# Modulation units issued later: two per item in layer 0, four in layer 1, five per head in layer 2, four per head in layer 3

## The chip, the cores and the metric

The program runs on one core of one Trainium2 chip. The metric is the device time of one execution in microseconds (us), as the median of the runs.

## What is computed

The reference is a stack of two blocks of two layers each, over 256 image tokens and 256 context tokens of width 1024. Layers 0 and 1 belong to the first block (grouped attention, pooling and Fourier branches, SwiGLU), layers 2 and 3 to the second (differential attention over 8 heads, a depthwise convolution of 31 taps, gates, squared-ReLU MLP). Before everything a layer does, it needs its *modulation*: six vectors of 1024 numbers, computed from a conditioning vector alone.

```python
for i in range(DEPTH):
    ...
    mod_x = (sc @ w_ada[i] + b_ada[i])[:, None, :]      # w_ada[i]: 1024 x 6144
    sh1, sc1, ga1, sh2, sc2, ga2 = jnp.split(mod_x, 6, axis=-1)
    hx = rms_norm(x, g_mix[i]) * (1.0 + sc1) + sh1
    ...                                                  # attention and the other branches
    x = x + ga1 * (mx @ w_out[i])
    fx = rms_norm(x, g_ffn[i]) * (1.0 + sc2) + sh2
    x = x + ga2 * swiglu(fx, w_gate_up[i], w_down[i])
```

In the second block an attention weight is the difference of two softmax maps per head, and q and k of a head are normalised and rotated first. The last layer of each block updates the image tokens only, so that layers 1 and 3 have 256 query columns and layers 0 and 2 have 512.

## The kernel before

`plan()` writes all steps into one list; each engine then walks this list and emits its own part, so that an engine's order of work is the order of the list, and semaphores do the rest. Layers are counted from 0 here, as in the code.

**Weights.** Every weight block is 128 columns by up to 1024 rows (step `wb`). ScalarE rounds it into `w_hi` (line 1272), VectorE makes the rest `w_lo` (line 1517), and TensorE does three matmuls for each 128 rows (lines 1130 to 1132). All weights come through one ring of four buffers `raw`, in one stream of DMAs that SyncE issues in order (line 1074); an entry is fetched when the entry four places ahead of it has been consumed.

**Modulation units.** The matrix `w_ada` of a layer is read in 3 banks of 16 units; a unit is one ring entry of 512 KB and four short matmuls (line 1110), which read it as it lands. A bank sums up in a PSUM bank of its own and is then transposed and finished by VectorE (lines 1566 to 1580). The plan says where the units stand: `layer_first` takes a number of units per attention item in layers 0 and 1 (`pump`), `layer_second` takes up to 10 per head in layer 2 and distributes them over a head's groups by the table `UNITS_IN`, and the norm before the MLP (`gap`) and the MLPs of layers 0 and 1 take the remaining 8 and 8 of one bank. Before the change every unit of layer 3 was done by the end of layer 2, and layer 3 had none.

**Attention.** `attend` interleaves the items (128 queries of one head). Of one item the TensorE order is: scores `S` (line 1207, into `sc`), transposes `T` of the item before (line 1217, into `pt`), fill work, the values product `PV` of the item before (line 1231 or 1233, into `pv`), more fill work. Scores go through VectorE (maximum, line 1726), ScalarE (exponential, line 1413) and VectorE (normalising: line 1741 in the first block, 1747 in the second) before they can be transposed. ScalarE copies the transposes (line 1422). The fill work of a head in layers 2 and 3 is a table of `groups`, 8 for four items in layer 2 and 4 for two items in layer 3: the next head's q, k and v blocks, their norms, and the end of the head before.

**The norms of q and k.** `query_sum` (called through `q_norm`) is a matmul of squares into `aux` (line 1161), a rotation matmul (line 1165), two ScalarE reads of `aux` (lines 1372 and 1374; the second one says that `aux` is free), and VectorE work. `qk_norm` (called through `k_norm`) is a matmul into the same `aux` (line 1140), which must wait for that, and a rotation matmul (line 1145). Its result is spread by 16 short matmuls (line 1155), which the rope of k (line 1701) reads.

**The end of a head.** Behind the spread rows come `PV`, the transpose of v (line 1172), the transposes of the finished head (line 1239), and the first scores of the next head. VectorE does taps of the convolution in between (line 1790). In layers 1 and 3 VectorE may hold a block's `w_lo` back (`split_due`) until the next block or the next modulation unit stands in the list.

Of the kernel before, what the change touches and what calls it, by code (L numbers as in the profile page):

```python
# [29 lines left out]
NT = 512  # L30
# [12 lines left out]
UNIT = 1024  # L43
ADA_BANKS = 3
LAYERS = 4
UNITS_IN = (0, 1, 1, 1, 1, 2, 2, 2)
LAM_INIT = [0.8 - 0.6 * float(np.exp(-0.3 * i)) for i in range(2)]


# [48 lines left out]
def plan():  # L98
# [9 lines left out]
    def signal(name, n=1):  # L108
        c[name] = c.get(name, 0) + n
        return name, c[name]  # L110

    def take(resource, slots, release):
        n = used.get(resource, 0)
        used[resource] = n + 1
        slot = n % slots
        before = last.get((resource, slot))
        last[resource, slot] = release
        return slot, before
# [7 lines left out]
    def step(kind, **kw):  # L126
        s = Step(kind=kind, i=counts.get(kind, 0), **kw)
        counts[kind] = s.i + 1
        steps.append(s)
        return s  # L130

    def after(name):
        return name, c.get(name, 0)
# [28 lines left out]

    def turn_place(s, q):

        if q.layer == 2:
            s.pt, s.pt_free = "pv", last.get(("pv", 0))
            last["pv", 0] = signal("turn_read")
        else:
            s.pt, s.pt_free = take("pt", 2, signal("turn_read"))
# [79 lines left out]
    def turn_probs(item):  # L249

        s = step("T", item=item)
        s.pt = []
        for h in range(2 if item.first else 1):
            ev = signal("pt_read")
            pt, free = take("pt", 2 if item.first or item.layer == 3 else 1, ev)
            pts, pts_free = take("pts", 2, None)
            s.pt.append(Step(bank=pt, free=free, ev=ev, slot=pts, slot_free=pts_free))
        last["e", item.e] = s.pt[-1].ev
        item.pt = s.pt
# [49 lines left out]
    def transpose(src, made, v_slot, v_free):  # L309

        s = step("tt", src=src, n=made.n, ready=made.rel, slot=v_slot, slot_free=v_free)
        s.ev = signal("pt_read")
        s.pt, s.pt_free = take("pt", 1 if made.layer == 2 else 2, s.ev)
        last[src, 0] = s.ev
        return s

# [19 lines left out]
    def ada_list(layer, banks=range(ADA_BANKS)):  # L336
        return [(layer, b, h, k) for b in banks for h in range(2) for k in range(KD)]
# [252 lines left out]
    def layer_second(layer, ada_head=(), first=(), gap=()):  # L590
# [29 lines left out]
        def conv_gate(t):  # L620
            g = w("w_cg", t, n, "sg", func=ACT.Sigmoid)
            g.qg, g.qg_free = take("sgl", 2, None)
            glu.append(g)

        def conv_value(t):
            g = glu[t]
            glu[t] = w("w_ca", t, n, "glu", other=g, free=last.get(("cz", 0)))
            last["sgl", g.qg] = glu[t].rel
# [131 lines left out]
        ada_left = [lambda a=a: ada(*a, psum="pt") for a in ada_head]  # L760
        q_block, k_block, q_norm, q_done, v_block, k_norm, k_made, k_done, v_turn = head_work(0)
# [14 lines left out]
        for h in range(8):  # L776
            its = q_items(False, h % 2, h % 2, h % 2, h, both, (held["kr", h].done, held["qr", h].done, held["vt", h].ev),
                          held["qr", h].norm)
            for it in its:
                it.layer = layer  # L780
                it.oslot = h % 2


            def mark(h=h):
                held["o", h - 1] = after("o_ready")
            q_block, k_block, q_norm, q_done, v_block, k_norm, k_made, k_done, v_turn = head_work(h + 1) if h < 7 else [lambda: None] * 9
            total, scale, turn_back, low = out_norm(h - 1) if h else [lambda: None] * 4
            mark = mark if h else lambda: None
            if both:
                groups = [[q_block], [], [mark, q_norm, q_done, k_block], [total], [k_norm, k_made, v_block, k_done],  # L790
                          [scale, v_turn], [turn_back, low], []]
            else:
                groups = [[q_block], [k_block, q_norm, q_done], [mark, total, k_norm, k_made, v_block, k_done, scale],
                          [v_turn, turn_back, low]]
            if h < 2:
                if both:
                    groups[6].append(lambda h=h: conv_gate(2 + h))
                    groups[7].append(lambda h=h: conv_value(2 + h))
                else:
                    groups[3].append(lambda h=h: conv_pair(2 + h))  # L800
            if h == 6:
                groups[-1].append(conv_add)
            if h == 7:
                g, p = conv_gate_of, conv_product
                if both:
                    parts = [[g(0), conv_mean, conv_centre], [conv_squares, g(1), conv_rstd], [conv_scale, g(2)], [g(3)],
                             [p(0), g(4)], [p(1), g(5)], [p(2), g(6)], [p(3), g(7)]]
                else:
                    parts = [[g(0), conv_mean, conv_centre, conv_squares, g(1), conv_rstd], [conv_scale, g(2), g(3)],
                             [p(0), g(4), p(1), g(5)], [p(2), g(6), p(3), g(7)]]  # L810
                for a, b in zip(groups, parts):
                    a += b
            ada_now = ada_left[:10]
            ada_left = ada_left[len(ada_now):]
            for j, g in enumerate(groups):
                slots = (7 - h) * len(groups) - j - 1
                if slots > 0:
                    g.append(lambda slots=slots: conv_taps(taps_due(slots, len(groups))))
                a, b = sum(UNITS_IN[:j]), sum(UNITS_IN[:j + 1])
                g += ada_now[a:b]  # L820
            attend(its, [lambda g=g: [f() for f in g] for g in groups])
            last["kT", h % 2] = after("scores_done")

            last["v", h % 2] = ("pv_done", c.get("pv_done", 0) + 1)
        attend_last()
        held["o", 7] = after("o_ready")
        total, scale, turn_back, low = out_norm(7)
# [15 lines left out]
        s = step("merge", n=n)  # L843
# [7 lines left out]
        for m in range(KD):  # L851
            s = wb(layer, "w_out2", m, "act", 0, KD, n, "resid", gate=16)
# [8 lines left out]
    r = rstd(D, NT, after("square_added"))  # L861
# [1 line left out]
        ada(*a)  # L863
    newton(r)
    step("lam")
    layer_first(0, ada_list(0, [1, 2]) + ada_list(1, [0]), 3, ada_list(1, [1])[:8], r)
    ffn(0, NT, ada_list(1, [1])[8:], NT)
    layer_first(1, ada_list(1, [2]), 2, ada_list(2, [0])[:8])
    ffn(1, NX, ada_list(2, [0])[8:], NT)
    layer_second(2, ada_list(2, [1, 2]) + ada_list(3)[:40], gap=ada_list(3)[40:])  # L870
    ffn(2, NT, [], NT)
    layer_second(3)
    ffn(3, NX, [], 0)


# [21 lines left out]
    r = 0  # L897
# [6 lines left out]


PLAN = plan()


# [1079 lines left out]
```

How the kernel before makes its waits and increments, by code:

```python
        def wait(eng, what):  # L1033
            if what is not None and what[1] > 0:
                eng.wait_ge(S[what[0]], what[1])
# [1 line left out]
        def wait_landed(eng, r):  # L1038
            eng.wait_ge(landed[r % RAW], 16 * (r // RAW + 1))
# [7 lines left out]
        @block.sync  # L1047
# [11 lines left out]
                    continue  # L1059
                if r == RAW:
                    sp.dma_start(x[:, :, :], xin).then_inc(S["x_in"], 16)
                    sp.dma_start(consts[:, 0:5 * P], const[:, 0:5 * P]).then_inc(S["const_in"], 16)
                if r == 16:
                    sp.dma_start(consts[:, 5 * P:], const[:, 5 * P:]).then_inc(S["const_in"], 16)
                    sp.dma_start(small[:, :, :], wsmall).then_inc(S["small_in"], 16)
                if r >= RAW:
                    before = raw_entries[r - RAW]
                    if before[0] == "w":
                        sp.wait_ge(S["lo_ready"], before[1] + 1)
                    else:
                        sp.wait_ge(S["ada_used"], before[1].used[1])
                n = UNIT if kind == "ada" else blocks[what][3] * P
                src = stream[offset:offset + P * n].rearrange("(p n) -> p n", p=P)
                sp.dma_start(raw[:, r % RAW, 0:n], src).then_inc(landed[r % RAW], 16)
                offset += P * n
                r += 1
            for s in steps[-KD:]:
                wait(sp, s.rel)
                sp.dma_start(out[s.m * P:(s.m + 1) * P, :], x[:, s.m, 0:NX]).then_inc(S["stored"], 16)
            sp.wait_ge(S["stored"], 16 * KD)
```

## Time and profile before

| what | value |
|---|---|
| median of 3 runs | 2478.14 us (2475.3 to 2478.62) |
| profiled execution, its own time | 2479.97 us |
| its span | 2478.2 us |
| TensorE matmul busy | 2331.5 us, 94% |
| TensorE weight loads busy | 1897.6 us, 77% |
| VectorE busy | 1323.9 us, 53% |
| ScalarE busy | 1040.2 us, 42% |
| HBM read | 332.58 MB, 135 GB/s over the span |

PE is the matmul side of TensorE and PEld its weight loads, DVE is VectorE, ACT is ScalarE, SP is SyncE. Matmuls are pipelined: a row's duration holds the way through the array too, so what a group costs is read from its start to the start of the group behind it. Attention runs from about 90 to 208 us in layer 0, 675 to 745 in layer 1, 1047 to 1400 in layer 2 and 1975 to 2200 in layer 3. The granted clock (PEclk) is 1.00 at 2.4 GHz and 0.50 at 1.2 GHz.

### The profile page before, as it was taken

To read this page: it belongs to the slowest core of one execution; us is meant where nothing else is said; L and a number is where in the kernel's file an instruction comes from. 1 tells how busy PE (TensorE), PEld (TensorE's weight loads), DVE (VectorE), ACT (ScalarE), POOL (GpSimd) and SP (SyncE) were. 2 spreads that over 40 slices of the span, in tenths; PEclk is the share of its full clock that TensorE was granted. 3 is DMA by queue.
4 is the path that set the end of the run, shared out by engine and by line. 5 is a ranking of instruction groups with operands and counts; after the bars stand their busy time and mean duration, and the time that the engine had idled before them with its cause. 6 is when DMAs were issued, how large, how long until landed. Compare 5 with 4: busy or idle time off the path is not lost.

```text
span 2478.2 us, 35757 instructions
## 1 busy us (share of the span) xinstructions
PE 2331.5 (94%) x14174; PEld 1897.6 (77%) x14174; DVE 1323.9 (53%) x2254; ACT 1040.2 (42%) x1966; POOL 33.2 (1%) x40
## 2 busy tenths in 40 slices
PE   5999899999888998899999999899999899998999
PEld 2656688888657998767666787688888787798999
DVE  4444433333655555567776434444344578756665
ACT  3343422222544444444445523423323465664543
POOL 0300000000200000000000000000000000000000
PEclk9999999999999999899999999899999899999999
DMA  7465433323345665144554322323223221154554
GB/s 268 155 223 168 142 110 102 110 94 111 111 166 183 194 207 182 65 145 155 194 182 151 110 95 85 126 96 107 89 94 103 74 96 60 60 162 145 173 189 141
DMA packets 94885, 335.96 MB, mean 136 GB/s; under 512 B 10624, under 2 KB 12672, under 8 KB 94464
## 3 DMA queue, kind: packets, MB, share of 16 engines
q1 hardware_dynamic: 94720, 333.67, 40.9%
q8 instruction: 114, 1.87, 0.3%
q14 instruction: 51, 0.42, 0.1%
HBM read 332.58 MB, written 1.05 MB: 135 GB/s over the span
## 4 chain that ended last, share of the span: by engine, by line
PE 85%; DVE 5%; ACT 4%; DMA 4%; issue 2%; SPq 0%; ACTq 0%; DVEq 0%
PE out L1130 24%; PE out L1131 24%; PE out L1132 24%; DMA raw<-stream 4%; PE sc L1207 2%; PE pt L1217 1%; PE pt L1110 1%; PE pv L1233 1%; PE aux L1155 1%; PE out L1110 1%; ACT w_hi L1272 1%; PE pv L1231 1%; PE aux L1140 1%; PE sc L1110 1%; DVE w_lo L1517 1%
## 5 line engine op out<-in xcount | busy, mean ns | idle before, releaser
L1130 PE MATMUL out<-act_hi,w_lo 128*128 128x512 f32 (+1 forms) x2272 | 804.2, 354 | 35.0 <-DVE act_lo L1681 26.4
L1131 PE MATMUL out<-act_lo,w_hi 128*128 128x512 f32 (+1 forms) x2272 | 789.7, 348 | 0.0
L1132 PE MATMUL out<-act_hi,w_hi 128*128 128x512 f32 (+1 forms) x2272 | 788.5, 347 | 0.0
L1272 ACT CAST w_hi<-raw 128x1024 fp32r<-128x1024 f32 (+2 forms) x444 | 452.3, 1021 | 428.2 <-PE out L1132 418.6
L1517 DVE TENSOR_TENSOR w_lo<-raw,w_hi 128x1024 fp32r<-128x1024 f32 (+2 forms) x444 | 529.8, 1196 | 172.5 <-ACT w_hi L1272 171.8
L1130 PEld LDWEIGHTS out<-act_hi,w_lo 128*128 128x128 f32 x2272 | 438.8, 193 | 100.2 <-issue 42.7
L1132 PEld LDWEIGHTS out<-act_hi,w_hi 128*128 128x128 f32 x2272 | 438.1, 193 | 53.0
L1131 PEld LDWEIGHTS out<-act_lo,w_hi 128*128 128x128 f32 x2272 | 438.6, 193 | 50.3
L1130 PE MATMUL out<-mix_hi,w_lo 128*128 128x512 f32 (+1 forms) x1120 | 377.8, 337 | 4.4 <-DVE mix_lo L1754 1.7
L1131 PE MATMUL out<-mix_lo,w_hi 128*128 128x512 f32 (+1 forms) x1120 | 376.3, 336 | 0.0
L1132 PE MATMUL out<-mix_hi,w_hi 128*128 128x512 f32 (+1 forms) x1120 | 376.2, 336 | 0.0
L1130 PEld LDWEIGHTS out<-mix_hi,w_lo 128*128 128x128 f32 x1120 | 212.5, 190 | 30.5 <-issue 4.7
L1132 PEld LDWEIGHTS out<-mix_hi,w_hi 128*128 128x128 f32 x1120 | 212.5, 190 | 21.9
L1131 PEld LDWEIGHTS out<-mix_lo,w_hi 128*128 128x128 f32 x1120 | 212.6, 190 | 21.7
L1616 DVE SCALAR_TENSOR_TENSOR x<-out,mods,x 128x256 f32<-128x256 f32 x216 | 97.8, 480 | 199.0 <-PE out L1132 199.0
L1591 DVE TENSOR_TENSOR e_t<-e_t,out 128x512 f32<-128x512 f32 (+1 forms) x44 | 24.4, 554 | 230.1 <-PE out L1132 225.1
L1790 DVE SCALAR_TENSOR_TENSOR stage<-stage,vecs 128x512 f32<-128x512 f32 (+1 forms) x240 | 139.1, 613 | 1.8
L1413 ACT ACTIVATE e_t<-sc,smax,rq 128x512 f32<-128x512 f32 (+1 forms) x144 | 100.8, 706 | 55.7 <-DVE smax L1729 55.3
L1598 DVE TENSOR_TENSOR e_t<-e_t,out 128x512 f32<-128x512 f32 (+1 forms) x64 | 35.5, 555 | 138.0 <-ACT e_t L1336 137.9
L1336 ACT ACTIVATE e_t<-out 128x512 f32<-128x512 f32 (+1 forms) x64 | 31.5, 493 | 146.1 <-PE out L1132 146.1
L1726 DVE TENSOR_REDUCE smax<-sc 128x2 f32<-128x1024 f32 (+1 forms) x72 | 75.1, 1042 | 29.9 <-PE sc L1207 29.4
L1422 ACT COPY p_t<-pt 128x512 f32<-128x512 f32 (+1 forms) x96 | 47.1, 517 | 100.0 <-PE pt L1217 100.0
(193 smaller groups left out, 1886.1 us busy)
## 6 DMA issues: line engine op xcount, KB each, us to landing
raw<-stream SPq DMA_DIRECT2D x604, 512.0 KB, 3.6
raw<-stream SPq DMA_DIRECT2D x16, 384.0 KB, 3.1
raw<-stream SPq DMA_DIRECT2D x16, 256.0 KB, 2.7
x<-xin SPq DMA_DIRECT2D x1, 2048.0 KB, 11.8
consts<-const SPq DMA_DIRECT2D x1, 1344.0 KB, 8.0
x<-ctx SPq DMA_DIRECT2D x1, 1024.0 KB, 5.9
out<-x SPq DMA_DIRECT2D x8, 128.0 KB, 1.7
consts<-const SPq DMA_DIRECT2D x1, 320.0 KB, 11.6
```

The source lines that it names most:

```text
L1110: ins = nc.tensor.matmul(ada_bank[32 * q:32 * q + 2, s.half * NX:(s.half + 1) * NX], cv[:, s.layer // 2, s.k, :], u[:, q], start=(s.k == 0 ...
L1130: nc.tensor.matmul(ps, wl, xh, start=(k == 0), stop=False)
L1131: nc.tensor.matmul(ps, wh, xl, start=False, stop=False)
L1132: ins = nc.tensor.matmul(ps, wh, xh, start=False, stop=(k == s.nk - 1))
L1207: ins = nc.tensor.matmul(scb[h][:, 0:b - a], q_t[rows, it.qslot, it.c0:it.c0 + P], k_t[rows, it.kslot, a:b], start=True, stop=True)
L1272: nc.scalar.copy(w_hi[:, number % HL, 0:n], raw[:, place[number] % RAW, 0:n]).then_inc(S["hi_ready"], 1)
L1413: ins = nc.scalar.activation(e_t[:, 2 * it.e + h, 0:n], scb[h][:, 0:n], ACT.Exp, scale=rq[:, it.qslot, j:j + 1], bias=smax[:, it.e, h:h + ...
L1422: nc.scalar.copy(p_t[:, t.slot, 0:n // P, :], ptb[t.bank][:, 0:n].rearrange("p (t n) -> p t n", n=P))\
L1517: nc.vector.tensor_tensor(w_lo[:, number % HL, 0:n], raw[:, place[number] % RAW, 0:n], w_hi[:, number % HL, 0:n].bitcast(F32), ALU.subtrac ...
L1616: ins = nc.vector.scalar_tensor_tensor(out=x[:, s.m, cols], in0=ps[:, cols], scalar=mods[:, s.layer, s.gate + s.m, h:h + 1], in1=x[:, s.m, ...
L1726: link(nc.vector.reduce_max(smax[:, it.e, :], scores_of[:, :, 0:n], AX_X))
L1790: nc.vector.scalar_tensor_tensor(out=dst, in0=src, scalar=w, in1=dst, op0=ALU.mult, op1=ALU.add)\
```

## The change

Every bank after the first ones is read later: in sum 16 units (one bank of layer 1) leave the attention of layer 0 for layer 1's, and 32 units (two banks of layer 3) leave the attention of layer 2 for layer 3's. The table of layer 2 gets 5 units a head instead of 10, layer 3 gets a table of its own with one unit in each of a head's four groups, and the units of layers 2 and 3 now both take the PSUM bank `pt1`. So layer 3 has one bank left for the transposes, the rotations of q and k go to the back half of `pv`, and the norm of the next q moves one group later, behind the scores of the second item.

```diff
--- before.py
+++ after.py
@@ -43,7 +43,7 @@
 UNIT = 1024
 ADA_BANKS = 3
 LAYERS = 4
-UNITS_IN = (0, 1, 1, 1, 1, 2, 2, 2)
+UNITS_IN = {2: (0, 1, 0, 1, 0, 1, 1, 1), 3: (1, 1, 1, 1)}
 LAM_INIT = [0.8 - 0.6 * float(np.exp(-0.3 * i)) for i in range(2)]
 
 
@@ -162,7 +162,7 @@
 
     def turn_place(s, q):
 
-        if q.layer == 2:
+        if q.layer >= 2:
             s.pt, s.pt_free = "pv", last.get(("pv", 0))
             last["pv", 0] = signal("turn_read")
         else:
@@ -252,7 +252,7 @@
         s.pt = []
         for h in range(2 if item.first else 1):
             ev = signal("pt_read")
-            pt, free = take("pt", 2 if item.first or item.layer == 3 else 1, ev)
+            pt, free = take("pt", 2 if item.first else 1, ev)
             pts, pts_free = take("pts", 2, None)
             s.pt.append(Step(bank=pt, free=free, ev=ev, slot=pts, slot_free=pts_free))
         last["e", item.e] = s.pt[-1].ev
@@ -310,7 +310,7 @@
 
         s = step("tt", src=src, n=made.n, ready=made.rel, slot=v_slot, slot_free=v_free)
         s.ev = signal("pt_read")
-        s.pt, s.pt_free = take("pt", 1 if made.layer == 2 else 2, s.ev)
+        s.pt, s.pt_free = take("pt", 1 if made.layer >= 2 else 2, s.ev)
         last[src, 0] = s.ev
         return s
 
@@ -790,7 +790,7 @@
                 groups = [[q_block], [], [mark, q_norm, q_done, k_block], [total], [k_norm, k_made, v_block, k_done],
                           [scale, v_turn], [turn_back, low], []]
             else:
-                groups = [[q_block], [k_block, q_norm, q_done], [mark, total, k_norm, k_made, v_block, k_done, scale],
+                groups = [[q_block], [k_block], [mark, q_norm, total, q_done, k_norm, k_made, v_block, k_done, scale],
                           [v_turn, turn_back, low]]
             if h < 2:
                 if both:
@@ -810,13 +810,13 @@
                              [p(0), g(4), p(1), g(5)], [p(2), g(6), p(3), g(7)]]
                 for a, b in zip(groups, parts):
                     a += b
-            ada_now = ada_left[:10]
+            ada_now = ada_left[:sum(UNITS_IN[layer])]
             ada_left = ada_left[len(ada_now):]
             for j, g in enumerate(groups):
                 slots = (7 - h) * len(groups) - j - 1
                 if slots > 0:
                     g.append(lambda slots=slots: conv_taps(taps_due(slots, len(groups))))
-                a, b = sum(UNITS_IN[:j]), sum(UNITS_IN[:j + 1])
+                a, b = sum(UNITS_IN[layer][:j]), sum(UNITS_IN[layer][:j + 1])
                 g += ada_now[a:b]
             attend(its, [lambda g=g: [f() for f in g] for g in groups])
             last["kT", h % 2] = after("scores_done")
@@ -863,13 +863,13 @@
         ada(*a)
     newton(r)
     step("lam")
-    layer_first(0, ada_list(0, [1, 2]) + ada_list(1, [0]), 3, ada_list(1, [1])[:8], r)
-    ffn(0, NT, ada_list(1, [1])[8:], NT)
-    layer_first(1, ada_list(1, [2]), 2, ada_list(2, [0])[:8])
+    layer_first(0, ada_list(0, [1, 2]), 2, ada_list(1, [0])[:8], r)
+    ffn(0, NT, ada_list(1, [0])[8:], NT)
+    layer_first(1, ada_list(1, [1, 2]), 4, ada_list(2, [0])[:8])
     ffn(1, NX, ada_list(2, [0])[8:], NT)
-    layer_second(2, ada_list(2, [1, 2]) + ada_list(3)[:40], gap=ada_list(3)[40:])
+    layer_second(2, ada_list(2, [1, 2]) + ada_list(3, [0])[:8], gap=ada_list(3, [0])[8:])
     ffn(2, NT, [], NT)
-    layer_second(3)
+    layer_second(3, ada_list(3, [1, 2]))
     ffn(3, NX, [], 0)
```

The order of instructions below is that of one head in the middle of a layer. The first piece is TensorE in layer 3, around the second item of a head (line 1110 is a unit, 1161 and 1165 belong to the norm of q, 1140 and 1145 to that of k, 1207 are the scores, 1217 the transposes):

```order
 L1132 MATMUL out<-act_hi,w_hi 128x512
-L1161 MATMUL aux<-consts,sq 128x2 x2
-L1165 MATMUL pt<-qg,consts 128x256
+L1110 MATMUL pt<-raw,cv 2x256 x4
 L1207 MATMUL sc<-k_t,q_t 128x512 x2
 L1217 MATMUL pt<-consts,e_t 128x128 x4
+L1161 MATMUL aux<-consts,sq 128x2 x2
+L1165 MATMUL pv<-qg,consts 128x256
 L1140 MATMUL aux<-consts 128x2 x4
-L1145 MATMUL pt<-qg,consts 128x256
+L1145 MATMUL pv<-qg,consts 128x256
 L1130 MATMUL out<-act_hi,w_lo 128x512
```

The norm of q stood ahead of the scores and now stands directly ahead of the norm of k, with nothing of TensorE between the two. The same place on ScalarE (1413 are the exponentials of the second item, 1372 and 1374 read `aux`):

```order
+L1433 ACTIVATE o_t,o_ss<-pv 128x128
+L1434 COPY o_t<-pv 128x128
+L1422 COPY p_t<-pt 128x512
+L1413 ACTIVATE e_t,ssum<-sc,smax,rq 128x512 x2
 L1372 ACTIVATE q_y<-aux,eps 128x4
 L1374 ACTIVATE q_ms<-aux,eps 128x4
 L1375 ACTIVATE q_y<-q_y 128x4
 L1376 ACTIVATE q_sq<-q_y 128x4
-L1433 ACTIVATE o_t,o_ss<-pv 128x128
-L1434 COPY o_t<-pv 128x128
-L1422 COPY p_t<-pt 128x512
-L1413 ACTIVATE e_t,ssum<-sc,smax,rq 128x512 x2
```

The reads of `aux` moved from ahead of the exponentials to behind them. The end of a head in layer 3 on VectorE (1701 is the rope of k behind the spread rows, 1747 the normalising of the second item), before:

```order
L1669 SCALAR_TENSOR_TENSOR n_r<-n_sq,n_y 128x8
L1517 TENSOR_TENSOR w_lo<-raw,w_hi 128x1024
L1701 TENSOR_TENSOR k_t<-qg,aux 128x512
L1767 SCALAR_TENSOR_TENSOR o_sq<-o_ms,o_sq 128x2
L1768 SCALAR_TENSOR_TENSOR o_r<-o_sq,o_y 128x2
L1770 TENSOR_TENSOR consts<-consts,o_r 128x256
L1790 SCALAR_TENSOR_TENSOR stage<-stage,vecs 128x256 x3
L1744 RECIPROCAL srec<-ssum 128x1
```

and of the change:

```order
L1669 SCALAR_TENSOR_TENSOR n_r<-n_sq,n_y 128x8
L1701 TENSOR_TENSOR k_t<-qg,aux 128x512
L1767 SCALAR_TENSOR_TENSOR o_sq<-o_ms,o_sq 128x2
L1768 SCALAR_TENSOR_TENSOR o_r<-o_sq,o_y 128x2
L1770 TENSOR_TENSOR consts<-consts,o_r 128x256
L1790 SCALAR_TENSOR_TENSOR stage<-stage,vecs 128x256 x3
L1517 TENSOR_TENSOR w_lo<-raw,w_hi 128x1024
L1744 RECIPROCAL srec<-ssum 128x1
```

The `w_lo` of a block moved from ahead of the rope to between the taps and the normalising, since a unit now stands there. The end of a head in layer 2 on TensorE, before:

```order
L1155 MATMUL aux<-consts,n_r 64x128 x8
L1110 MATMUL pt<-raw,cv 2x256 x4
L1233 MATMUL pv<-v_t,p_t 128x128 x4
L1172 MATMUL pt<-consts,vf 128x128 x4
L1110 MATMUL pt<-raw,cv 2x256 x8
L1207 MATMUL sc<-k_t,q_t 128x256 x2
L1217 MATMUL pt<-consts,e_t 128x128 x2
L1239 MATMUL aux<-consts,o_t 128x128 x4
L1110 MATMUL pt<-raw,cv 2x256 x8
L1233 MATMUL pv<-v_t,p_t 128x128 x2
L1110 MATMUL pt<-raw,cv 2x256 x8
L1207 MATMUL sc<-k_t,q_t 128x512 x2
```

and of the change:

```order
L1155 MATMUL aux<-consts,n_r 64x128 x8
L1233 MATMUL pv<-v_t,p_t 128x128 x4
L1172 MATMUL pt<-consts,vf 128x128 x4
L1110 MATMUL pt<-raw,cv 2x256 x4
L1207 MATMUL sc<-k_t,q_t 128x256 x2
L1217 MATMUL pt<-consts,e_t 128x128 x2
L1239 MATMUL aux<-consts,o_t 128x128 x4
L1110 MATMUL pt<-raw,cv 2x256 x4
L1233 MATMUL pv<-v_t,p_t 128x128 x2
L1110 MATMUL pt<-raw,cv 2x256 x4
L1207 MATMUL sc<-k_t,q_t 128x512 x2
```

Seven units stood behind the spread rows of a head, and three are left.

## Rows read from the trace of the kernel before

**Rows 1.** Windows: us; busy of PE, PEld, DVE, ACT, POOL; clock; DMA share; GB/s

```profile
90.50:208.00 117.50, 112.25 (x912) 61.72 (x914) 59.28 (x139) 52.36 (x142) 7.04 (x9) 0.99 0.68 228
675.00:745.00 70.00, 62.60 (x506) 39.34 (x507) 37.48 (x84) 32.71 (x83) 4.88 (x6) 0.98 0.47 158
1047.50:1400.00 352.50, 335.59 (x2126) 238.29 (x2126) 241.70 (x473) 183.03 (x458) 0.00 (x0) 0.97 0.46 155
1975.00:2200.00 225.00, 215.24 (x1395) 179.75 (x1394) 171.07 (x388) 137.02 (x329) 0.00 (x0) 0.98 0.25 81
0.00:43.00 43.00, 20.68 (x146) 5.93 (x146) 10.97 (x26) 11.20 (x19) 0.20 (x4) 1.00 0.92 346
```
**Rows 2.** Timeline, layer 2: a modulation unit and the next PE group

```profile
1292.04 0.61 PE L1110 MATMUL pt<-raw,cv 128*2 128x256 f32 x8
1292.59 1.16 PE L1233 MATMUL pv<-v_t,p_t 128*128 128x128 f32 x8
```
**Rows 3.** Waits of PE, layer 2 attention: total us, times, longest

```profile
PE pt L1110 <- DMA raw<-stream: 7.6, 8, 3.3
PE pt L1217 <- DVE e_t L1747: 6.2, 3, 3.4
PE pt L1110 <- DVE stage L1566: 2.6, 1, 2.6
```
**Rows 4.** Timeline, layer 3: second item of a head

```profile
2090.88 0.50 PE L1161 MATMUL aux<-consts,sq 128*128 128x2 f32 x4
...
2091.85 1.13 PE L1207 MATMUL sc<-k_t,q_t 64*128 64x512 f32 x4
...
2092.91 0.66 PE L1217 MATMUL pt<-consts,e_t 128*128 128x128 f32 x4
...
2093.40 0.95 PE L1140 MATMUL aux<-consts 128*128 128x2 f32 x8
...
2099.97 1.22 DVE L1517 TENSOR_TENSOR w_lo<-raw,w_hi 128x1024 fp32r<-128x1024 f32 x1
...
2100.29 1.09 PE L1155 MATMUL aux<-consts,n_r 128*64 128x128 f32 x16
```
**Rows 5.** Timeline, layer 2: scores of an item and the ScalarE read

```profile
1272.39 1.13 PE L1207 MATMUL sc<-k_t,q_t 64*128 64x512 f32 x4
...
1276.93 0.27 ACT L1374 ACTIVATE q_ms<-aux,eps 128x8 f32<-128x8 f32 x1
```
**Rows 6.** Timeline, layer 3: spread rows to transposes, end of a head

```profile
2076.25 1.09 PE L1155 MATMUL aux<-consts,n_r 128*64 128x128 f32 x16
...
2081.17 0.66 PE L1217 MATMUL pt<-consts,e_t 128*128 128x128 f32 x4 [0.81 <-DVE e_t L1747]
```
**Rows 7.** Timeline, layer 2: end of a head without a long wait

```profile
1291.02 1.09 PE L1155 MATMUL aux<-consts,n_r 128*64 128x128 f32 x16
...
1300.02 0.61 PE L1110 MATMUL pt<-raw,cv 128*2 128x256 f32 x8 [0.65 <-DMA raw<-stream]
...
1300.52 0.48 DVE L1747 SCALAR_TENSOR_TENSOR e_t<-e_t,srec 128x256 f32<-128x256 f32 x1
...
1301.63 0.44 PE L1217 MATMUL pt<-consts,e_t 128*128 128x128 f32 x2
```
**Rows 8.** Timeline, layer 2: end of a head with a long wait

```profile
1252.37 1.09 PE L1155 MATMUL aux<-consts,n_r 128*64 128x128 f32 x16
...
1265.57 0.44 PE L1217 MATMUL pt<-consts,e_t 128*128 128x128 f32 x2
```
**Rows 9.** Windows: eight us behind a single PE wait

```profile
255.40:263.40 8.00, 5.21 (x64) 2.88 (x64) 3.01 (x7) 3.43 (x9) 0.00 (x0) 1.00 0.68 229
1510.30:1518.30 8.00, 7.98 (x28) 6.47 (x29) 5.79 (x10) 3.73 (x7) 0.00 (x0) 0.79 0.22 65
```
**Rows 10.** Timeline, layer 1: scores of two items in a row

```profile
731.20 1.13 PE L1207 MATMUL sc<-k_t,q_t 64*128 64x512 f32 x4 [0.58 <-DVE q_t L1654]
...
736.46 1.13 PE L1207 MATMUL sc<-k_t,q_t 64*128 64x512 f32 x4
```

## The prediction, made before the changed kernel was run

> **What bounds the kernel now.** I read the windows of the four attention stretches first. PE is busy in nearly all of them: 112.3 of 117.5 us in layer 0, 62.6 of 70 in layer 1, 335.6 of 352.5 in layer 2, 215.2 of 225 in layer 3 [rows 1]. DVE has 171 of 225 us in layer 3 and ACT 137, so no other engine is the bound there, only single chains through them. The DMA engines have a share of 0.68 in layer 0, 0.46 in layer 2 and 0.25 in layer 3 [rows 1]: layer 3 has free bandwidth, but no idle PE. So a modulation unit costs PE its own time wherever it stands, unless it stands in a wait. From the start of a unit to the start of the group behind it are 0.55 us [rows 2], and I take 0.54. The change moves 48 units and drops none, and their own time cancels. What decides is which waits the moved units leave and which they make. The waits of PE in layer 2 are next: 7.6 us for units that had not landed, 2.6 us for a bank that had to be transposed, 6.2 us for normalised probabilities [rows 3]. The timeline of a head then shows the chains.
>
> **Layer 0: 16 units fewer.** 16 x 0.54 = 8.6 us. In the last items there is no fill work, and the chain from scores to transposes takes a little back. Result **-8**.
>
> **Layer 1: 16 units more.** +8.6 us. The shortest items are 5.26 us apart [rows 10]. With two more units that is 6.3 us for four units of 0.52 MB, 333 GB/s; the prologue moved 346 [rows 1], so the ring can just follow. I add 1 us for landing and 1 us for one more bank transposed, and take off 1.6 us, since of the waits there the one of 0.58 us for q [rows 10] and one for probabilities at the end stand behind a unit. Result **+9**; from +6 (waits filled, none made) to +16 (each item waits a further us for the ring).
> The Trainium skill (DMA: Bandwidth & Descriptors, Bandwidth) gives 341 GB/s for transfers of 1 MB and names about 358 as the share of the memory for one core. By it the ring follows as well, and the sum would lose the 1 us for landing.
>
> **Layer 2: 32 units fewer, 5 fewer in each of heads 0 to 6, 3 more in head 7.**
> - *The ends of heads 2 to 6.* Four of the seven units behind the spread rows go. But this end is not PE's alone. The rows end at 1292.11; then DVE and ACT work through the rope, taps, maximum, exponentials, the turned head and the normalising without a pause that a unit makes, until 1301.00 [rows 7]. So the next transposes can't start earlier than 8.95 us behind the rows, with however few units. Before, they start 9.5 us behind them in this head and 12.1 in another [rows 7, 8]. All ten us of waits for landing and transposing [rows 3] lie in the ends of these five heads: 2 us each, on top of about 8.2 that PE needs by itself (9.5 less two waits of about 0.6 [rows 7]), and in three of them the clock is low for a while. I take a gain of 1.9 us each (between 0.6 and 3.1), **-9.5**. The 2.2 us of removed units give nothing more: PE now needs 6.1 us and waits 2.9 us for the chain.
> - *Their middles* lose one unit each, 2.7 us, of which heads that already wait for probabilities [rows 3] keep some: **-2**. *Heads 0 and 1* end with two weight blocks, so PE bounds them: 10 x 0.54, less 1 us held at such waits, **-4.4**. *Head 7*: **+1.6**.
> - *The clock.* Behind a single wait of PE of 2.4 to 3.5 us the granted clock mostly falls to the lower level: of the eleven such waits behind the prologue ten show it. One without and one with it are given; 8 us at 0.79 have lost 1.7 us [rows 9]. The new wait of 2.9 us is broken in two by the next scores, so I take 1 us for each of five heads, **+5** (0 to 8).
>
> Together **-9.3**; between -18 and -3.
>
> **Layer 3: 32 units more.**
> - *Own time.* 32 x 0.54 = **+17.3**.
> - *The norm of k waits for the norm of q.* Both use `aux`, and TensorE may write line 1140 only when ACT has read q's sums (line 1374). Before, q's sums were made ahead of the scores, 2.5 us before line 1140 [rows 4], and ACT read them at once. Now ACT has the exponentials of the same item in its queue first, and these wait for DVE's maximum. Layer 2 has this order already: from the start of the scores to the end of the read of q's sums are 4.81 us (1272.39 to 1277.20) [rows 5], hidden there by a k block that stands between the two norms. In layer 3 no block stands there. From the start of the scores PE has 1.06 us of scores and 0.49 of transposes, then q's two groups, which before took 0.97 [rows 4]: 2.52 us. It waits 4.81 - 2.52 = 2.3 us, or 2.6 if q's last matmul takes no longer than k's does. I take 2.5 in each of heads 0 to 6: **+17.5**. Queued behind it are the norm of k and the v block (6.9 us from line 1140 to the spread rows [rows 4]), the rows and the end of the head, so nothing on PE can fill it. From below this is bounded by 0 (if ACT were done early, which the row excludes unless its maximum came sooner) and from above by 3.5.
> - *The end of a head.* Before, transposes start 3.8 us behind the rows, after a wait of 0.81 for DVE [rows 6]. The units there would fit into that wait by 0.8, but `w_lo` of 1.22 us [rows 4] now stands in DVE's queue ahead of the normalising; DVE comes 1.2 us later, PE 1.1. Nothing is filled: **+0.8** over five heads. In head 7 a unit stands in a wait: **-0.7**.
> - *The clock.* Seven single waits of 2.5 us with weight blocks behind them are just the case of rows 9: nine in ten of 1.7 us, 7 x 1.5 = **+10.5** (0 to 20).
>
> Together **+45.4**; between +27 and +60. The transposes' single bank costs nothing: its readers on ACT are done several us before it is needed again. The ring is not short either, with 7 entries in a head of 29 us.
>
> **The sum.** -8 + 9 - 9.3 + 45.4 = +37 us. On the profiled execution's own time of 2480 that is 2517; the median of the runs is 2 us lower, so 2515. All other stages have the same units as before.
>
> **The rivals.** A change below 0.2% (5 us) is taken as none, about what the runs can tell apart.
> 1. *Units in layer 3 are free, and layer 2 is rid of its load (faster).* In layer 3 PEld is busy 180 of 225 us [rows 1], so a fifth of the stretch has no weight load. If units went in there, layer 3 would get 0 to +5 instead of 17 for them, and if besides the read of q's sums were in time (it decides from a wait below about 1 us on), layer 2 with its ten us of waits and its units would carry the sum: -8 + 7 - 18 + 5 = -14, 2464. Against it: a head is 24.0 us from rows to rows [rows 4, 6], and in it PE has no wait but the 0.81 [rows 6]. 12 in 100.
> The Trainium skill (Perfetto Trace Analysis, Identifying the Most-Contended Engine) says just this, that busy matmuls are no good measure and that the busy share of weight loads is. By it layer 3 has a fifth of PE free. PE's 215 us beside PEld's 180 are loads that end before the matmul ahead of them does, not free time; the trace speaks against taking the rule here, and by it the sum would be 17 us lower.
> 2. *The wait at k's norm is hidden or stays under a us, but units cost their time.* -8 + 9 - 9.3 + 17.3 + 3 = +12, 2490. For it: DVE is idle when the scores end, so the maximum can't be late; it would need ACT to take it early. 12 in 100.
> 3. *Nothing measurable:* rival 2 with the best case of layer 2 (-18), 2481. 6 in 100.
> 4. *The ring in layer 1 is too short.* Its items wait for landing as layer 2's ends do, 2 us in half of the eight: +8 on my sum, 2523. 10 in 100.
>
> My forecast has 60 in 100, the range of its own terms being 2497 to 2532. With the rivals, 8 in 10 lie between 2488 and 2533. Faster 0.13, same 0.06, slower 0.81.
>
> **What would show it.** In the profile of the changed kernel: PE waits at line 1140 in layer 3 for ACT's q_ms, seven times, 2 to 2.7 us; the clock of that stretch falls from 0.98 to about 0.94; heads there are 29 to 31 us apart instead of 24. In layer 2 the waits for landing vanish, transposes wait for DVE's e_t about 1.9 us and scores for ACT's e_t about 1 in five heads, and the transposes start 8.9 to 9.0 us behind the rows. Layer 0 is 8 us shorter, layer 1 9 us longer. The forecast is wrong if ACT reads q's sums before the exponentials end, if the clock stays high behind waits of 2.5 us, or if heads in layer 3 grow by less than 3 us.

## The result: 1.8% slower

| | after | before, on the same chip |
|---|---|---|
| median | 2523.18 us (2519.24 to 2527.92, 4 runs) | 2476.72 us (2475.23 to 2478.62, 4 runs) |
| ratio | 1.0184, 95% interval 1.0168 to 1.0199 | |
| profiled execution, its own time | 2527.92 us | 2479.97 us |
| its span, mean granted clock | 2526.1 us, 0.966 | 2478.2 us, 0.975 |

The change costs 46.5 us; +37 were predicted (2515, range 2488 to 2533). The medians below count every run, but the ratios leave out three that ran at a far lower clock: one of `before_reorder_only`, one of `units_l2_l3_order_kept` and one of the before beside it. The profile page of after says little of where the 46.5 us are. PE is busy 26 us more than before (2331.5 us), although it has the same 14174 matmuls, and the three other engines do the same work in the same time:

```profile
span 2526.1 us, 35757 instructions
PE 2357.8 (93%) x14174; PEld 1914.3 (76%) x14174; DVE 1324.0 (52%) x2254; ACT 1042.2 (41%) x1966; POOL 33.2 (1%) x40
```

So I cut both spans where the first and the last scores of each layer's attention start. The windows of after, with columns as in [rows 1]; the first, third, fifth and last row are the attention of layers 0 to 3:

```profile
91.20:195.20 104.00, 101.11 (x742) 56.98 (x742) 53.89 (x125) 48.78 (x131) 6.99 (x9) 0.98 0.50 167
195.20:674.20 479.00, 460.73 (x2168) 372.50 (x2164) 194.02 (x273) 149.95 (x222) 7.66 (x9) 0.97 0.33 110
674.20:744.70 70.50, 62.42 (x554) 36.89 (x554) 34.54 (x76) 28.68 (x74) 4.95 (x6) 0.98 0.64 228
744.70:1058.70 314.00, 290.33 (x2224) 266.35 (x2220) 167.06 (x249) 137.37 (x215) 0.00 (x0) 0.95 0.52 174
1058.70:1387.10 328.40, 308.01 (x1795) 227.83 (x1794) 234.12 (x458) 175.37 (x443) 0.00 (x0) 0.96 0.32 109
1387.10:1974.00 586.90, 561.39 (x2578) 460.42 (x2574) 260.08 (x366) 198.34 (x292) 0.00 (x0) 0.98 0.30 99
1974.00:2219.90 245.90, 223.09 (x1439) 170.42 (x1438) 160.17 (x364) 120.92 (x293) 0.00 (x0) 0.92 0.34 122
```

The same windows of before are 110.7, 473.7, 61.6, 311.1, 340.5, 587.4 and 197.4 us long, at a clock of 0.98, 0.99, 0.97, 0.96, 0.97, 0.97 and 0.98. The differences are -6.7, +5.3, +8.9, +2.9, -12.1, -0.5 and +48.5 us, and with +1.6 for what lies ahead of and behind them they make the 47.9 us between the spans. Layer 3 alone is as large as the whole result. Its clock fell from 0.98 to 0.92, and TensorE stands idle in 23 of 246 us instead of 6 of 197.

What PE waited for, after (total us, times, longest): the first row is layer 3's attention, the next two are layer 2's, the last is layer 1's with its last item (674 to 753 us).

```profile
PE aux L1140 <- ACT q_ms L1374: 16.4, 7, 2.3
...
PE pt L1217 <- DVE e_t L1747: 16.5, 10, 3.4
PE sc L1207 <- ACT e_t L1413: 1.9, 4, 0.5
...
PE out L1110 <- DMA raw<-stream: 4.7, 6, 1.3
```

The first row is new and is the wait that was predicted, seven times. In layer 2 the waits for landing and for transposing of [rows 3] are gone, and the wait for normalised probabilities has taken their place. The fourth row was predicted at 1 us.

The timeline of a head in layer 3 shows the new wait. This is the place of [rows 4]:

```profile
2118.80 0.61 PE L1110 MATMUL pt<-raw,cv 128*2 128x256 f32 x8
...
2119.34 1.13 PE L1207 MATMUL sc<-k_t,q_t 64*128 64x512 f32 x4
...
2120.40 0.66 PE L1217 MATMUL pt<-consts,e_t 128*128 128x128 f32 x4
...
2120.52 1.22 DVE L1726 TENSOR_REDUCE smax<-sc 128x2 f32<-128x1024 f32 x1 [1.02 <-PE sc L1207]
...
2120.90 0.51 PE L1161 MATMUL aux<-consts,sq 128*128 128x2 f32 x4
...
2121.26 0.68 PE L1165 MATMUL pv<-qg,consts 128*128 128x256 f32 x2
...
2122.06 0.78 ACT L1413 ACTIVATE e_t<-sc,smax,rq 128x512 f32<-128x512 f32 x1 [0.37 <-DVE smax L1729]
...
2122.83 0.77 ACT L1413 ACTIVATE e_t<-sc,smax,rq 128x512 f32<-128x512 f32 x1
...
2123.87 0.26 ACT L1374 ACTIVATE q_ms<-aux,eps 128x4 f32<-128x4 f32 x1
...
2124.28 1.02 PE L1140 MATMUL aux<-consts 128*128 128x2 f32 x8 [2.34 <-ACT q_ms L1374]
```

The sums of q stand in `aux` at 2121.4, but ScalarE comes to them at 2123.6, behind the two exponentials, and these started only after VectorE's maximum. From the start of the scores to the end of line 1374 are 4.79 us; the prediction took 4.81 from layer 2 [rows 5]. All seven waits measure 2.34 or 2.35 us.

Windows of eight us behind two of the seven waits:

```profile
1989.80:1997.80 8.00, 7.99 (x26) 6.75 (x27) 3.03 (x10) 1.87 (x6) 0.00 (x0) 0.61 0.02 6
2026.30:2034.30 8.00, 8.00 (x32) 6.72 (x33) 3.12 (x11) 2.32 (x9) 0.00 (x0) 0.79 0.03 11
```

Behind the other five waits one such window shows 0.61 and four show 0.79. So all seven waits are followed by a stretch at the lower level, and two of them by one nearly twice as long as in [rows 9].

The ends of heads. The first two rows are layer 2's (spread rows and transposes, as [rows 7, 8]), the other two layer 3's (as [rows 6]):

```profile
1258.22 1.09 PE L1155 MATMUL aux<-consts,n_r 128*64 128x128 f32 x16
...
1268.26 0.44 PE L1217 MATMUL pt<-consts,e_t 128*128 128x128 f32 x2 [1.65 <-DVE e_t L1747]
...
2132.83 1.09 PE L1155 MATMUL aux<-consts,n_r 128*64 128x128 f32 x16
...
2138.88 0.66 PE L1217 MATMUL pt<-consts,e_t 128*128 128x128 f32 x4 [1.07 <-DVE e_t L1747]
```

In layer 2 the transposes start 8.95 us behind the end of the rows (1259.31 to 1268.26), just what the chain of [rows 7] was said to allow. Three of the five ends of heads 2 to 6 measure this; the first takes 9.61 us and the last only 7.89, so 8.95 is no floor for every head. In layer 3 they start 4.96 us behind them instead of 3.83.

### The profile page after: what moved, and what is told of

Read it like the earlier page. It is cut to its first block, busy times and chain, and to the rows that moved or that the text cites. A ratio compares the mean times of both kernels' runs of the same rounds, so it can differ in the third digit from the quotient of the medians.

```text
span 2526.1 us, 35757 instructions
## 1 busy us (share of the span) xinstructions
PE 2357.8 (93%) x14174; PEld 1914.3 (76%) x14174; DVE 1324.0 (52%) x2254; ACT 1042.2 (41%) x1966; POOL 33.2 (1%) x40
## 4 chain that ended last, share of the span: by engine, by line
PE 82%; DVE 7%; ACT 5%; DMA 3%; issue 3%; SPq 0%; ACTq 0%; DVEq 0%
PE out L1130 23%; PE out L1131 23%; PE out L1132 23%; DMA raw<-stream 3%; PE sc L1207 2%; PE pt L1217 1%; ACT w_hi L1272 1%; PE aux L1140 1%; PE aux L1155 1%; PE pv L1233 1%; ACT e_t L1413 1%; DVE w_lo L1517 1%; PE pt L1110 1%; DVE smax L1726 1%; DVE stage L1790 1%
## 5 line engine op out<-in xcount | busy, mean ns | idle before, releaser
L1347 ACT ACTIVATE qg<-x 128x512 f32<-128x512 f32 (+1 forms) x56 | 32.3, 578 | 134.9 <-DVE x L1616 133.9
## 6 DMA issues: line engine op xcount, KB each, us to landing
consts<-const SPq DMA_DIRECT2D x1, 320.0 KB, 11.3
```

The costliest lines, as they stand in the source:

```text
L1347: nc.scalar.activation(qg[:, s.qg, 0:s.n], x[:, s.m, 0:s.n], ACT.Square).then_inc(S["square_done"], 1)
```

## The experiments

All labels name kernels that differ from before or after only by what is shown. `qorder_fixed`, `before_reorder_only`, `early_read` and `units_l0_l1_only` ran on one chip, beside a before of 2476.14 us (13 runs). The others ran on two further chips, each beside runs of before there (2478.45 and 2477.07 us), so times of different groups are compared through their own before.

**1. The norm of q ahead of the scores again (`qorder_fixed`).** Against after; all 48 units stay where the change puts them. The rotations leave `pv` for the transpose bank again; experiment 3 leaves them in `pv`.

```diff
-        if q.layer >= 2:
+        if q.layer == 2:
             s.pt, s.pt_free = "pv", last.get(("pv", 0))
...
-            s.pt, s.pt_free = take("pt", 2, signal("turn_read"))
+            s.pt, s.pt_free = take("pt", 1 if q.layer == 3 else 2, signal("turn_read"))
...
-  groups = [[q_block], [k_block], [mark, q_norm, total, q_done, k_norm, k_made, v_block, k_done, scale],
+  groups = [[q_block], [k_block, q_norm, q_done], [mark, total, k_norm, k_made, v_block, k_done, scale],
```

> The changed kernel, but in layer 3 the norm of q stands ahead of the scores again (in the one transpose bank), all units as in the change. Theory (the norm of k waits for ScalarE's read behind the exponentials, and the clock falls behind that wait): the seven waits of 2.3 us at line 1140 go (16 us), and with them most of seven low-clock stretches (10 to 15 us), so 2490 to 2500 us. Rival (the single transpose bank or the units' DMAs make the loss in layer 3): those stay, so 2515 to 2523 us.

Measured: 2494.08 us (2492.76 to 2498.45), ratio 1.0075 (1.0060 to 1.0090). Of the 46 us, 18 are left. The window of layer 3's attention, and what PE waited for in it:

```profile
1969.60:2184.40 214.80, 205.50 (x1439) 158.30 (x1438) 158.25 (x364) 117.93 (x292) 0.00 (x0) 1.00 0.39 140
```

```profile
PE pt L1217 <- DVE e_t L1747: 4.1, 5, 1.1
...
PE aux L1155 <- DVE n_r L1669: 2.6, 6, 0.8
```

The wait for q_ms is gone, and with it the low stretches: the clock is 1.00 over the window. The heads are 26.9 us apart in the middle of the layer, 30.7 in after and 24.0 in before. So the order costs 31.1 us in this window, and four units a head cost 2.9 us: 2.2 of their own and 0.7 more. The timeline points to `w_lo` for the 0.7: it now stands on VectorE ahead of the maximum of the second item's scores and of the normalising: over the window the spread rows wait 2.6 us for `n_r` instead of 1.0 in before, the transposes 4.1 us for `e_t` instead of 2.8. No experiment takes this part away alone.

**2. The new order and its banks alone (`before_reorder_only`).** Against before; no unit moves.

```diff
-        if q.layer == 2:
+        if q.layer >= 2:
...
-            pt, free = take("pt", 2 if item.first or item.layer == 3 else 1, ev)
+            pt, free = take("pt", 2 if item.first else 1, ev)
...
-        s.pt, s.pt_free = take("pt", 1 if made.layer == 2 else 2, s.ev)
+        s.pt, s.pt_free = take("pt", 1 if made.layer >= 2 else 2, s.ev)
...
-  groups = [[q_block], [k_block, q_norm, q_done], [mark, total, k_norm, k_made, v_block, k_done, scale],
+  groups = [[q_block], [k_block], [mark, q_norm, total, q_done, k_norm, k_made, v_block, k_done, scale],
```

> The kernel before with only layer 3's order and banks of the change, all units where they were before. Theory: 16 us of waits at line 1140 plus 10 to 15 us of low clock, so 2500 to 2508 us. Rival (the loss in layer 3 comes from the units there): 2477 us, no change.

Measured: 2515.44 us, ratio 1.0157 (1.0140 to 1.0174). Waits of PE and window in layer 3's attention:

```profile
PE aux L1140 <- ACT q_ms L1374: 15.9, 7, 2.3
```

```profile
1975.80:2206.10 230.30, 209.04 (x1200) 168.65 (x1198) 157.94 (x361) 119.14 (x292) 0.00 (x0) 0.91 0.19 62
```

The mechanism stands without a single moved unit: 15.9 us of waits, and a window 32.9 us longer than before's. The other 17 us agree with the clock: 0.91 instead of 0.98 over 230 us is some 17 us of full clock. I had expected 2500 to 2508 from waits of 17 us and some 10 of clock, so the clock's price was too low. Outside this window the span grew by 2.7 us more, at places where nothing differs.

**3. The order of TensorE kept, ScalarE's read ahead of the exponentials (`early_read`).** Against after. If the wait is for ScalarE's place in its queue and not for TensorE's own order, it must vanish here.

```diff
-    def attend(items, fills, units=0):
+    def attend(items, fills, units=0, early=None):
...
+            if early and j == 1:
+                early()
...
-  groups = [[q_block], [k_block], [mark, q_norm, total, q_done, k_norm, k_made, v_block, k_done, scale],
+  groups = [[q_block], [k_block], [mark, total, q_done, k_norm, k_made, v_block, k_done, scale],
...
-            attend(its, [lambda g=g: [f() for f in g] for g in groups])
+            attend(its, [lambda g=g: [f() for f in g] for g in groups], early=None if both else q_norm)
```

> The changed kernel, but ScalarE has the two reads of q's sums ahead of the exponentials of the same item; TensorE's order is that of the change. Theory: the wait at line 1140 falls from 2.3 us to about 0.6, 12 us in all, and the low clock behind it goes too (10 to 15 us): 2495 to 2502 us. Rival (TensorE's order or the banks matter, not ScalarE's queue): 2520 us or more.

Measured: 2495.09 us, ratio 1.0070 (1.0054 to 1.0087). In this kernel line 1142 is after's 1140, and 1376 its 1374:

```profile
PE aux L1142 <- ACT q_ms L1376: 2.4, 7, 0.3
```

```profile
1969.90:2186.60 216.70, 207.85 (x1441) 158.69 (x1440) 158.61 (x364) 118.80 (x292) 0.00 (x0) 0.99 0.39 139
```

The same wait is there seven times, but of 0.35 us, and none of the seven is followed by a low stretch; the one that is left stands behind a wait of 2.55 us for VectorE's `stage`. It is ScalarE's queue that made the wait. All fourteen of these waits of 2.3 us (seven each in after and `before_reorder_only`) are followed by a low stretch, and none of the seven of 0.35 us. A head in the middle of the layer is 27.07 us long, 0.17 us longer than in `qorder_fixed`.

**4. Only the units of layers 0 and 1 (`units_l0_l1_only`).** Against before.

```diff
-    layer_first(0, ada_list(0, [1, 2]) + ada_list(1, [0]), 3, ada_list(1, [1])[:8], r)
-    ffn(0, NT, ada_list(1, [1])[8:], NT)
-    layer_first(1, ada_list(1, [2]), 2, ada_list(2, [0])[:8])
+    layer_first(0, ada_list(0, [1, 2]), 2, ada_list(1, [0])[:8], r)
+    ffn(0, NT, ada_list(1, [0])[8:], NT)
+    layer_first(1, ada_list(1, [1, 2]), 4, ada_list(2, [0])[:8])
```

> The kernel before with only the units of layers 0 and 1 moved as in the change. By the terms of the prediction (-8 and +9): +1, 2478 us. By the stretches of the changed kernel's trace up to layer 2 (11 us longer, 5 of them between the attention of layer 0 and that of layer 1): 2485 to 2488 us, if that part is caused by the move and is not chance of one execution.

Measured: 2483.50 us (10 runs), ratio 1.0024 (1.0013 to 1.0036), +6 to +7 us. The attention of layer 0 is 8.2 us shorter than before's, that of layer 1 is 9.0 longer; the prediction's -8 and +9 hold. In the stretch behind layer 1, 2.6 us are added: two more units in the last item (1.1 us), and in its units a wait for landing of 1.9 us that before does not have. The stretch between the two attentions has one unit less than before's, and yet took 479.6 us instead of 473.7. Its window, and before's:

```profile
192.90:672.50 479.60, 460.77 (x2167) 372.32 (x2163) 193.86 (x273) 149.84 (x222) 7.64 (x9) 0.97 0.33 110
```

```profile
201.20:674.90 473.70, 454.39 (x2174) 368.17 (x2171) 194.22 (x273) 149.85 (x222) 7.63 (x9) 0.99 0.35 113
```

PE is busy 6.4 us more with seven matmuls less: that is the clock, 0.97 and 0.99. Two windows of after and the one of before that answers to the first show where it falls:

```profile
200.70:207.50 6.80, 4.99 (x17) 3.88 (x18) 2.31 (x6) 1.39 (x3) 0.00 (x0) 0.50 0.30 101
251.90:258.70 6.80, 6.80 (x48) 4.18 (x47) 0.34 (x2) 0.73 (x4) 0.00 (x0) 0.50 0.49 143
```

```profile
201.00:209.00 8.00, 4.96 (x60) 2.44 (x52) 4.44 (x13) 4.02 (x13) 0.00 (x0) 1.00 0.86 284
```

At the first place, the end of layer 0's attention, PE is partly idle in both kernels. The second stands behind the wait of 2.43 us whose 8 us in before are the row at 1.00 in [rows 9]. Two low stretches of 6.8 us cost up to 6.8 us, as much as the whole difference. But they don't come from the moved units. Twelve of the thirteen profiles, seven of them of kernels with the units of before, have both: the ten us that begin 4 us behind the start of the last scores have a clock of 0.66 or 0.83, and the 8 us behind the wait one of 0.57 or 0.79. Only the one profile of before has 1.00 at both. The stretch took 473.7 to 477.6 us in the eight profiles of kernels with the units of before, and 476.5 to 479.7 us in the five with them moved, 2.3 us apart in the mean. With these 2.3 the four stretches make +5.7 us (-8.2 + 2.3 + 9.0 + 2.6), which agrees with the runs. What makes the 2.3 us is open.

**5. A single bank for the transposes (`before_single_bank`).** Against before: `take("pt", 1, ...)` in layer 3 for transposes, rotations and the transpose of v; order and units stay.

> The kernel before with one transpose bank in layer 3 for probabilities, v and the rotations, order and units as before. Theory (the banks cost nothing, the order does): 2474 to 2479 us, no change. Rival (part of the 39 us of the run with reorder and banks alone comes from the banks): 2482 us or more, with waits of PE for ScalarE's copies of the transposes.

Measured: 2477.29 us beside 2478.45, ratio 0.9997 (0.9985 to 1.0009). The bank costs nothing, as predicted.

**6. VectorE keeps its hold on `w_lo` at a unit (`qorder_fixed_split_later`).** Against `qorder_fixed`. This was to win back the 0.7 us a head.

```diff
-                elif s.kind == "ada":
+                elif s.kind == "ada" and s.layer < 3:
                     split_due()
```

> The run with q's order mended, and a unit in layer 3 no longer releases a held w_lo, so that the w_lo waits for the next block as before. Theory (w_lo ahead of the normalising makes the units at a head's end cost their full time): heads in layer 3 go from 26.9 us to about 26.1, -5 us in all, 2489 us. Rival (DVE isn't what the transposes wait for; the units cost their own time alone): 2494 us, no change, or more, if the ring now waits for w_lo.

Measured: 2513.74 us, ratio 1.0137 (1.0116 to 1.0157) against its own before of 2478.45. That is 35 us where `qorder_fixed` has 18 against its own, so some 15 (by the ratios) to 17 us slower, where I had expected a gain. PE's first wait in layer 3, and the longest one:

```profile
PE pt L1110 <- DMA raw<-stream: 22.3, 11, 4.5
```

```profile
2094.51 1.03 PE L1110 MATMUL pt<-raw,cv 128*2 128x256 f32 x8 [4.50 <-DMA raw<-stream]
```

`w_lo` is also what frees the block's ring entry. Held back until the next block, it holds the transfers behind it, and the units, which read their entry as it lands, stand waiting. The rival that the ring waits for `w_lo` came true, and whether the early `w_lo` costs the 0.7 us a head can't be read from this run; whatever it costs, it buys far more.

**7. The two parts of the units added up (`units_l2_l3_order_kept`).** Against `qorder_fixed`, with the three lines of layers 0 and 1 as in before.

> Layers 0 and 1 as in the kernel before; layers 2 and 3 with the units of the change, but q's norm ahead of the scores. If the parts add up: the run with q's order mended (+18) less the run with layers 0 and 1 alone (+7) is +11, 2489 us. If the parts interact (the ring or the clock), it differs from that by 5 us or more.

Measured: 2489.66 us beside 2477.07, ratio 1.0043 (1.0028 to 1.0058). With the 0.24% of experiment 4 this makes 0.67%, and both together measured 0.75%: within the intervals they add up.

**8. Other places for the ten units of layer 2 (three tables on before).** If the ends of the heads carry ten us of waits, fewer units there might give them back without moving a unit out of the layer.

```diff
-UNITS_IN = (0, 1, 1, 1, 1, 2, 2, 2)
+UNITS_IN = (0, 2, 1, 2, 1, 1, 1, 2)     # before_table_mid
+UNITS_IN = (0, 2, 1, 1, 2, 1, 1, 2)     # before_table_step
+UNITS_IN = (0, 1, 2, 1, 1, 2, 1, 2)     # before_table_late
```

> The kernel before, only layer 2's table is (0, 2, 1, 2, 1, 1, 1, 2): five of ten units stand ahead of the spread rows instead of three. If the end of a head is bounded by the chain through VectorE (9 us behind the rows) and the waits for landing go: an end of 9.0 instead of 11.1 us, 1.1 us more in the middle, so 1 us less in each of five heads plus the clock: 2465 to 2472 us. If the units at the end were free and only their time counts: 1.1 us more in seven heads, 2484 us.

> As the run before, with (0, 2, 1, 1, 2, 1, 1, 2): one unit moved ahead of the rows, one from the last but one groups to the group of the rows. Theory of the chain: an end of 9.0 to 9.5 us, 0.5 more in the middle, 1.2 us less in each of five heads and less low clock: 2464 to 2471 us. Rival as there: 2480 us.

> The same kernel as the run with the table (0, 2, 1, 1, 2, 1, 1, 2), once more: 4 us faster than the kernel before if the first measurement holds (2470 to 2475 us), no difference if it was chance.

> The kernel before with the table (0, 1, 2, 1, 1, 2, 1, 2): again four units ahead of the rows, but the two behind v's transpose stay together. If only the count ahead of the rows matters, as the run with (0, 2, 1, 1, 2, 1, 1, 2), -4 us; if two units together at the end wait for landing, an end of 9.5 us and -1 to 0 us.

| kernel | median, us | before, us | ratio |
|---|---|---|---|
| `before_table_mid` | 2478.45 | 2478.45 | 0.9998 (0.9987 to 1.0009) |
| `before_table_step` | 2474.82 | 2478.45 | 0.9983 (0.9973 to 0.9994) |
| `before_table_step_again`, the same kernel | 2477.05 | 2477.07 | 0.9999 (0.9990 to 1.0008) |
| `before_table_late` | 2484.64 | 2477.07 | 1.0027 (1.0017 to 1.0037) |

PE's waits in layer 2's attention in `before_table_step`:

```profile
PE pt L1217 <- DVE e_t L1747: 10.7, 7, 3.2
PE pt L1110 <- DVE stage L1566: 3.3, 2, 3.0
```

The waits for landing are gone (7.6 us in before), but those for probabilities have grown from 6.2 to 10.7 us. What one engine no longer waits for, the next link of the same chain asks. The gain of the first measurement was not seen in the second, so none of the tables is better than before beyond doubt, and no kernel here beats it. The expected 2465 to 2472 and 2464 to 2471 us were missed. `before_table_late` is 7 to 8 us slower, where I had expected -4 or -1 to 0: PE waits in its layer 2 4.5 us for landing, 7.2 for a bank to be transposed and 7.9 for probabilities, 19.6 in all beside 16.4 in before.

## Why the prediction was right, and where its sizes were off

- **What bounds it.** PE does, and a unit costs its own time: 0.54 us from the unit at 2118.80 to the scores at 2119.34, as in [rows 2]. In `qorder_fixed` layer 3's PE busy time grew by 14.5 us, although the clock was 1.00 instead of 0.98, while PEld's grew by 1.5. This speaks against rival 1 and against the rule of the Trainium skill (Perfetto Trace Analysis, Identifying the Most-Contended Engine) beside it, as far as that goes by weight loads: PEld was busy in 157 of 197 us, and yet no unit fitted in for nothing.
- **Layer 3, own time (+17.3).** 30 units stand inside the window, 16.2 us. Right.
- **Layer 3, the norm of k waits (+17.5).** Measured 7 x 2.34 = 16.4. Right in place, cause and size (the working gave 2.3, I took 2.5): experiments 1 to 3 take it away or bring it alone, and `early_read` shows that ScalarE's queue is the cause. Rival 2 falls with it.
- **Layer 3, the clock (+10.5).** This is the term that was mis-sized. 0.08 of 245.9 us less 0.02 of 197.4 is some 16 us. The seven windows of eight us alone have lost 14.6 us. I had taken nine in ten waits with 1.7 us each; all seven show it, and two of them lose 3.1 us. The terms for the units and the wait were 1.1 us too high each, which hides part of it.
- **Layer 3, the end of a head (+0.8 over five heads).** The transposes came 1.1 us later, as worked out. Without the long wait (`qorder_fixed`) four units cost 0.7 us a head beyond their own time, some 4 us more than I had for it, and the spread rows (line 1155) wait for `n_r` too. I had missed this second link; in after it has no wait, since the wait at line 1140 comes first.
- **Layer 2 (-9.3).** Measured -12.1 in its attention, inside -18 to -3. The five ends took 44.4 us instead of 55.7, a gain of 11.3 where I said 9.5; all the rest gave 0.8 where I said -0.2. The 8.95 us behind the rows held to the hundredth in three ends, but the last took 7.89, where the prediction says that they can't start earlier. Where it holds, it is why fewer units gave so little. Transposes wait 1.65 us in the head shown where I said 1.9, scores 0.48 where I said 1.
- **Layer 0 (-8).** -6.7 in after, -8.2 in experiment 4. The stretch behind it grew by 5.3 us in the profiled execution, half of the miss, and no term of mine stood for it. By experiment 4 some 3 us of that are no effect of the change: the one profile of before has no low clock at two places there where the twelve others have it. About 2 us of the move's own stay, which the prediction lacked.
- **Layer 1 (+9), and the ring.** Up to its last scores +8.9, made of 6.6 us of PE's own time and 3.3 us of waits for landing, less 1.0 us of waits for q and line 1161 that went. The last item adds 2.5 us (two units, and 1.4 us of landing). That is 11.4 us: PE waited 4.7 us for landing, not 1. So rival 4 had the mechanism half right, at 4.7 us instead of its 8 beyond the one that I took. That its 2523 us is the measured median is chance. By the rates of the Trainium skill (DMA: Bandwidth & Descriptors, Bandwidth) the ring would have followed; the window moved 228 GB/s, far under them, and units waited all the same. Whether a deeper ring would end this wasn't tried.
- **The sum by parts.** In ratios: units of layers 0 and 1 +0.24%, of layers 2 and 3 +0.43%, the new order +1.09% on top of them: 1.84% less the 0.75% of `qorder_fixed`. Alone on before the order measured +1.57%. In layer 3's window the two agree, +31.1 and +32.9 us, and over the profiled spans too, +33.0 and +35.6. The medians, which come from different executions and in part from another chip, make it 27 and 39 us; what sets them apart stays open.
- **The miss.** The spans grew by 47.9 us where the terms make 37.1. The terms were too low by 3.1 us for layer 3, 2.4 for layer 1 with its last item, 1.3 for layer 0, 5.3 for the stretch behind it and 1.5 for the others; layer 2 gained 2.8 more than forecast and hides as much. That the sum came so near is partly luck. Its own range of 2497 to 2532 is no sum of the bounds given for layers 1 to 3 either; those would make 2485 to 2543.

## What to carry to other kernels

When a step moves in one list that every engine walks, look at its place in each engine's queue. Here TensorE lost 0.35 us a head by doing the norm of q later, but ScalarE's read of the shared bank fell behind two exponentials, and the next writer of that bank had to wait. In this kernel a repeated wait of 2.3 us on the engine that bounds it has to be counted about twice (16.4 us of waits, some 16 us of clock); one of 0.35 us costs only itself. Take a place at its average over several profiles where you can: the one profile of before was 2.7 us shorter than seven others with the same work in a stretch that the change hardly touches. And before work is moved out of a stretch to rid it of waits, work out what the chain behind it still needs.

## What was not expected of the hardware

- Each of seven single waits of 2.34 us on TensorE, in a stretch that was otherwise full, was followed by 1.2 GHz for a while (clock 0.61 or 0.79 over the next 8 us); seven waits of 0.35 us at the same place were not, with a clock of 0.99 over the layer.
- The length of a wait doesn't settle this alone. Behind the wait of 2.43 us of [rows 9] the clock stayed at 1.00 in the profile of before and fell in the other twelve. The same wait of 2.61 us (line 1140 for VectorE's `stage`, in the last head of layer 3) ends at 2161.53 in before and at 2174.91 in `qorder_fixed`; the 8 us behind it:

```profile
2161.50:2169.50 8.00, 7.22 (x37) 6.93 (x38) 5.17 (x13) 6.93 (x15) 0.00 (x0) 0.58 0.20 68
2174.90:2182.90 8.00, 7.66 (x65) 7.02 (x66) 5.66 (x14) 6.66 (x14) 0.00 (x0) 1.00 0.47 166
```

- Two profiles of one and the same kernel (`before_table_step` and its repeat) have spans of 2466.4 and 2478.1 us at clocks of 0.979 and 0.969. Their layer 2 windows have the same waits, and differ only by the clock:

```profile
1045.70:1377.40 331.70, 316.35 (x2069) 226.80 (x2068) 236.38 (x464) 175.06 (x442) 0.00 (x0) 0.99 0.48 162
```

```profile
1051.00:1387.60 336.60, 321.14 (x2069) 229.22 (x2068) 236.60 (x464) 175.14 (x442) 0.00 (x0) 0.97 0.47 159
```

So a gain of 4 us that one comparison shows may be gone in the next, and a single profile can't place differences of that size.
